# Opening rebuilt, bias rows in 16 transfers instead of 48, and odd prompt heads' transposes copied by VectorE

## The reference

```python
for layer in range(2):
    x = x + 0.5 * swiglu(rms_norm(x, g1), w_gate, w_up, w_down)      # FFN 2816
    h = rms_norm(x, g)
    y = mla_mixer(h, ...) if layer == 0 else sliding_window_gqa(h, kv, rel_bias, sinks)
    x = x + y
    x = x + 0.5 * swiglu(rms_norm(x, g2), w_gate2, w_up2, w_down2)
    if layer == 0:
        kv = rms_norm(x, kv_norm) @ w_kv_shared
y = rms_norm(x, final_norm)
```

## Time and profile before

| what | value |
|---|---|
| median of 3 runs | 2559.46 us (2558.42 to 2562.18) |
| the profiled execution | 2553.65 us, its span 2551.8 us |
| TensorE busy | 2463.2 us, 97% of the span, 16448 matmuls |
| VectorE, ScalarE, GpSimd busy | 46%, 30%, 35% |
| chain that ended last | TensorE 89%, VectorE 5%, ScalarE 2%, issue 2%, GpSimd 1%, SyncE's queue 1%, DMA 1% |
| TensorE's longest waits | 15.4 us (VectorE, `wa`), 11.4 us (GpSimd, `wa`), 4.4 us (VectorE, `split`), 2.7 us (VectorE, `split`) |

### The profile page before, as it was taken

One profiled execution on the slowest core, in us unless ns is written; L12 is line 12 of the kernel. 1 busy time (PEld: TensorE's weight loads), 2 busy tenths in 40 slices (PEclk: granted clock), 3 DMA queues, 4 the chain that ended last, 5 costly groups with the idle time before them and its releaser, 6 DMA issues.

```text
span 2551.8 us, 42418 instructions
## 1 busy us (share of the span) xinstructions
PE 2463.2 (97%) x16448; PEld 2348.0 (92%) x16448; DVE 1161.3 (46%) x2375; ACT 763.5 (30%) x1496; POOL 893.3 (35%) x602
## 2 busy tenths in 40 slices
PE   6999999999999999999999899999999999999997
PEld 6999999987666999999999899999996899999997
DVE  6443434656355353434345334343455454434435
ACT  4222222422246222121214322212145442222223
POOL 3423333444113333333323433333355243333332
PEclk9999999999999999999999999999999999999998
DMA  4312123244242122222221322222222122222211
GB/s 144 95 59 92 59 90 75 85 151 157 87 142 87 53 81 75 74 74 74 74 74 34 125 75 74 74 74 74 74 104 100 42 75 92 66 82 69 79 49 42
DMA packets 73311, 210.80 MB, mean 83 GB/s; under 512 B 8385, under 2 KB 22753, under 8 KB 72449
## 3 DMA queue, kind: packets, MB, share of 16 engines
q1 hardware_dynamic: 73216, 209.55, 25.9%
HBM read 191.22 MB, written 18.30 MB: 82 GB/s over the span
## 4 chain that ended last, share of the span: by engine, by line
PE 89%; DVE 5%; issue 2%; ACT 2%; POOL 1%; SPq 1%; DMA 1%; DVEq 0%; ACTq 0%; POOLq 0%
PE psa L355 17%; PE psa L356 17%; PE psa L357 17%; PE psb L355 10%; PE psb L356 10%; PE psb L357 10%; DVE split L436 1%; PE psb L980 1%; PE psa L1116 1%; PE psa L949 1%; PE psb L1135 1%; PE psb L1123 1%; SPq L1923 1%; DVE work L403 1%; PE psa L950 1%
## 5 line engine op out<-in xcount | busy, mean ns | idle before, releaser
L355 PE MATMUL psa<-split,wa 128*128 128x320 f32 (+1 forms) x3072 | 954.2, 311 | 48.2 <-DVE wa L2069 15.4
L357 PE MATMUL psa<-split,wa 128*128 128x320 f32 x3056 | 943.3, 309 | 0.0
L356 PE MATMUL psa<-split,wa 128*128 128x320 f32 x3056 | 943.2, 309 | 0.0
L342 POOL TENSOR_TENSOR wb<-raw,wb 128x1024 fp32r<-128x1024 f32 (+1 forms) x100 | 237.5, 2375 | 1193.4 <-ACT wb L334 1193.4
L355 PEld LDWEIGHTS psa<-split,wa 128*128 128x128 f32 x3072 | 580.3, 189 | 53.5 <-DVE wa L2069 15.4
L356 PEld LDWEIGHTS psa<-split,wa 128*128 128x128 f32 x3056 | 576.5, 189 | 1.3 <-issue 0.6
L357 PEld LDWEIGHTS psa<-split,wa 128*128 128x128 f32 x3056 | 576.1, 189 | 0.0
L342 POOL TENSOR_TENSOR wa<-raw,wa 128x1024 fp32r<-128x1024 f32 x207 | 494.0, 2407 | 172.3 <-ACT wa L334 172.3
L355 PE MATMUL psb<-acts,wb 128*128 128x320 f32 x1440 | 446.4, 310 | 1.0 <-DVE xs L633 0.8
L633 DVE SCALAR_TENSOR_TENSOR xs<-psb,xs 128x320 f32<-128x320 f32 x720 | 341.4, 488 | 229.7 <-PE psb L357 229.7
L357 PE MATMUL psb<-acts,wb 128*128 128x320 f32 x1440 | 443.5, 308 | 0.0
(11 more groups left out here) (217 smaller groups left out, 2135.6 us busy)
## 6 DMA issues: line engine op xcount, KB each, us to landing
raw<-in_w SPq DMA_DIRECT2D x310, 512.0 KB, 3.9
park<-xs SPq DMA_DIRECT2D x2, 2560.0 KB, 9.1
work<-in_c_latT SPq DMA_DIRECT2D x8, 512.0 KB, 3.9
work<-in_c_lat SPq DMA_DIRECT2D x8, 512.0 KB, 3.6
xs<-in_x SPq DMA_DIRECT2D x2, 1280.0 KB, 9.1
xs<-park SPq DMA_DIRECT2D x1, 2560.0 KB, 13.4
xs<-park SPq DMA_DIRECT2D x2, 1280.0 KB, 5.6
y_out<-xs SPq DMA_DIRECT2D x8, 320.0 KB, 3.1
```

Source lines behind the costliest of these rows:

```text
L342: nc.gpsimd.tensor_tensor(lo[:, 0:n], raw[:, (p % RAW_SLOTS) * PIECE:(p % RAW_SLOTS) * PIECE + n], hi[:, 0:n].bitcast(F32), ALU.subtract). ...
L355: nc.tensor.matmul(ps, w[0], xx[1], start=first, stop=False)
L356: nc.tensor.matmul(ps, w[1], xx[0], start=False, stop=False)
L357: return nc.tensor.matmul(ps, w[0], xx[0], start=False, stop=last)
```

## The change

The opening: consts lose their last two columns and go first, alone; two weight pieces follow, then half 0 of x in two parts, half 1, the third and fourth piece, and only then `ones`. ScalarE copies one zeroed column first (`act_start`), splits two pieces, makes all 16 high parts of x and then all 16 squares, with the further splits between. VectorE (`dve_start`) splits the first five pieces and makes all adds; GpSimd begins with the sixth piece. `pe_bias` comes right after group (0,0), `dve_bias` ahead of VectorE's adds. The groups of unit 1 use the banks of `psb`, and both norm sums lie in group (1,0).

The bias rows: 8 transfers for the sampled rows, 4 heads each, and 8 for the band rows, 2 heads each. The prompt heads: the copy of odd tasks is VectorE's, with a semaphore of its own.

```diff
@@ semaphores, waits
-AHEAD = (0, 2)
+AHEAD = (2,)
-                eng.wait_ge(consts_in, 32)
-            if i % DT == 0:
-                eng.wait_ge(x_in[i // DT], 16)
+                eng.wait_ge(consts_in, 16)
+            if i % 4 == 0 and i < 12:
+                eng.wait_ge(x_in[i // 4], 16)
@@ new functions
+    def act_start(act):
+
+        act.wait_ge(warm_zero, 1)
+        nc.scalar.activation(consts[:, CONST_COLS - 1:CONST_COLS], consts[:, CONST_COLS - 2:CONST_COLS - 1], ACT.Copy).then_inc(warm_copy, 1)
+        split_hi(act, 0, 0)
+        split_hi(act, 0, 1)
+        for i in range(N_OUT):
+            norm_hi(act, 0, i)
+        for i in range(4):
+            norm_square(act, 0, i)
+        split_hi(act, 0, 2)
+        split_hi(act, 1, 0)
+        for i in range(4, DT):
+            norm_square(act, 0, i)
+        split_hi(act, 1, 1)
+        for i in range(DT, DT + 4):
+            norm_square(act, 0, i)
+        split_hi(act, 1, 2)
+        act_std(act, 0, 0)
+        for i in range(DT + 4, N_OUT):
+            norm_square(act, 0, i)
+        split_hi(act, 2, 0)
+        act_std(act, 0, 1)
+        split_hi(act, 2, 1)
+
+    def dve_start(dve):
+
+        nc.vector.memset(consts[:, CONST_COLS - 2:CONST_COLS - 1], 0.0).then_inc(warm_zero, 1)
+        early = [(0, 0), (0, 1), (0, 2), (1, 0), (1, 1)]
+
+        def split(p):
+            dve.wait_ge(w_hi, p + 1)
+            hi, lo = slots(*early[p])
+            nc.vector.tensor_tensor(lo, raw[:, lot(p % RAW_SLOTS, PIECE)], hi.bitcast(F32), ALU.subtract).then_inc(w_lo, 1)
+        split(0)
+        split(1)
+        for i in range(N_OUT):
+            dve_norm(dve, 0, i)
+        dve_bias(dve)
+        for i in range(DT):
+            norm_add(dve, 0, i)
+        for p in range(2, 5):
+            split(p)
+        for i in range(DT, N_OUT):
+            norm_add(dve, 0, i)
+        dve_rstd(dve, 0, 0)
@@ pe_gate_up, pe_ffn
-            bank_free = [(up_out, at(it, 8, GU * i + 2 * off + h - 1))]
+            bank_free = [(x_upd, BIAS_GROUPS), (n_std, 2 * h)][:h + 1] if i == 0 and it is None and off == 1 else [(up_out, at(it, 8, GU * i + 2 * off + h - 1))]
+        banks = psb[:, 2 * h:2 * h + 2, 0:HT] if i == 0 and it is None and off == 1 else psa[:, 2 * h:2 * h + 2, 0:HT]
-            if i != 2 and it is None and (off, h, k) in ((0, 1, 3), (1, 0, 1))[i == 3:]:
+            if i != 2 and it is None and (off, h, k) in (((1, 0, 0), (1, 0, 5)) if i == 0 else ((0, 1, 3), (1, 0, 1))[i == 3:]):
+                if i == 0 and (off, h) == (0, 0):
+                    pe_bias(pe)
@@ prompt heads
-                pe.wait_ge(a_ptd, t - 1)
+                pe.wait_ge(a_ptd_odd if t % 2 else a_ptd, t // 2)
-            pe.wait_ge(a_ptd, 2 * s + 2)
+            pe.wait_ge(a_ptd, s + 1)
+            pe.wait_ge(a_ptd_odd, s + 1)
             copy(2 * s)
-            copy(2 * s + 1)
+        def copy_odd(t):
+
+            dve.wait_ge(a_tr, t + 1)
+            if t >= 4:
+                dve.wait_ge(a_pv, t - 3)
+            n = P * (i_of(t) + 1)
+            nc.vector.tensor_copy(p_pt[:, t % 4, 0:n], psb[:, 1, 0:n]).then_inc(a_ptd_odd, 1)
@@ dve_prompt, after the two maxima of a step
+            copy_odd(2 * s + 1)
@@ transfers
-        sp.dma_start(consts[:, :], a["consts"]).then_inc(consts_in, 16)
-        sp.dma_start(ones[:, :], a["ones"]).then_inc(consts_in, 16)
-        for h in range(2):
-            sp.dma_start(x[:, :, half(h)], a["x"][:, :, half(h)]).then_inc(x_in[h], 16)
-            if h == 0:
-                load_piece(sp, 0, 0)
-                load_piece(sp, 0, 1)
+        sp.dma_start(consts[:, 0:CONST_COLS - 2], a["consts"][:, 0:CONST_COLS - 2]).then_inc(consts_in, 16)
+        load_piece(sp, 0, 0)
+        load_piece(sp, 0, 1)
+        for n, (d, h) in enumerate(((0, 0), (4, 0))):
+            sp.dma_start(x[:, d:d + 4, half(h)], a["x"][:, d:d + 4, half(h)]).then_inc(x_in[n], 16)
+        sp.dma_start(x[:, :, half(1)], a["x"][:, :, half(1)]).then_inc(x_in[2], 16)
         load_piece(sp, 0, 2)
         load_piece(sp, 1, 0)
+        sp.dma_start(ones[:, :], a["ones"]).then_inc(ones_in, 16)
-    def bias_rows(h):
-        first = h * CHUNK * RELS + CHUNK - 1
-        return a["l_park"][first:first + CHUNK * (RELS - 1)].rearrange("(q w) -> q w", w=RELS - 1)
+    def bias_rows(h, n, rows):
+
+        by_head = a["l_park"].rearrange("(h w) -> h w", w=CHUNK * RELS)[h:h + n, CHUNK - 1:CHUNK - 1 + rows * (RELS - 1)]
+        return by_head.rearrange("h (q w) -> h q w", w=RELS - 1)
-        for h in range(NH):
-            g, r = h // REP, h % REP
+        for g in range(KVH):
             for b2 in range(2):
-                sp.dma_start(w_sbias[b2 * HD + r * SQ:b2 * HD + (r + 1) * SQ, g, :], bias_rows(h)[0:SQ, 0:SKEYS]).then_inc(wsb_in, 16)
+                sp.dma_start(w_sbias[lot(b2, HD), g, :], bias_rows(REP * g, REP, SQ)[:, :, 0:SKEYS]).then_inc(wsb_in, 16)
-        for h in range(NH):
-            g, r = h // REP, h % REP
-            sp.dma_start(w_bias[lot(r % 2, CHUNK), 2 * g + r // 2, :], bias_rows(h)[:, 0:BAND]).then_inc(wb_in, 16)
+        for n in range(NH // 2):
+            sp.dma_start(w_bias[:, n, :], bias_rows(2 * n, 2, CHUNK)[:, :, 0:BAND]).then_inc(wb_in, 16)
@@ the engines' programs
-        pool_norm(pool, 0, 1)
-        pool.wait_ge(w_lo, 2)
-        split_lo(pool, 0, 2)
+        pool.wait_ge(w_lo, 5)
         pool_ffn(pool, 0)
```

More of the change, by code:

```diff
@@ L242, in program @@
         "consts_in", "bias_out", "parked", "x_back", "tables_in", "rope_in", "ident_in"))
-    x_in = [sem(f"x_in{h}") for h in range(2)]
+    x_in = [sem(f"x_in{h}") for h in range(3)]
+    ones_in = sem("ones_in")
     landed = [sem(f"w_landed{i}") for i in range(RAW_SLOTS)]
@@ L481, in act_table @@
             act.wait_ge(warmed, n)
+        else:
+            act.wait_ge(warm_copy, 1)
         nc.scalar.activation(consts[:, CONST_COLS - 1:CONST_COLS], eps, ACT.Sqrt).then_inc(warmed, 1)
@@ L506, in pe_gate_up @@
                 pe.wait_ge(n_lo, 16 * N_FFN[i] + h * DT + k + 1)
-            if i != 2 and it is None and (off, h, k) in ((0, 1, 3), (1, 0, 1))[i == 3:]:
+            if i != 2 and it is None and (off, h, k) in (((1, 0, 0), (1, 0, 5)) if i == 0 else ((0, 1, 3), (1, 0, 1))[i == 3:]):
                 if i:
                     pe.wait_ge(x_upd, OUT_BASE[f"ffn{i}"])
-                pe_norm_sum(pe, N_FFN[i], 1 - h)
+                if i == 0:
+                    pe.wait_ge(ones_in, 16)
+                pe_norm_sum(pe, N_FFN[i], k // 5 if i == 0 else 1 - h)
             xx = sp_hi[:, k, half(h)], sp_lo[:, k, half(h)]
-            mm3(psa[:, 2 * h, 0:HT], tiles(u, k), xx, k == 0, k == DT - 1)
-            last = mm3(psa[:, 2 * h + 1, 0:HT], tiles(u, DT + k), xx, k == 0, k == DT - 1)
+            mm3(banks[:, 0, :], tiles(u, k), xx, k == 0, k == DT - 1)
+            last = mm3(banks[:, 1, :], tiles(u, DT + k), xx, k == 0, k == DT - 1)
         last.then_inc(gu_mm, 1)
@@ L564, in tile_step @@
             follows = u0 + off + 1 < len(UNITS)
-            if it is None and off == 0 and i != 2:
+            if i == 0 and it is None and off < 2:
+                pass
+            elif it is None and off == 0 and i != 2:
                 act_std(act, N_FFN[i], 1)
@@ L570, in tile_step @@
             early = it is None and off == 0 and i != 2
-            if early:
+            if early and i:
                 split_hi(act, u0 + 1, 2)
@@ L586, in pool_ffn @@
         for off in range(2):
-            split_lo_unit(pool, u0 + off + 1)
+            for j in range(2 if i == 0 and off == 0 else 0, 3):
+                split_lo(pool, u0 + off + 1, j)
         with pool.Fori(0, FFN_LOOPS - 1) as it:
@@ L612, in dve_scaled @@
             dve.wait_ge(act_split, at(it, 8, n - 1))
-        nc.vector.tensor_tensor(gt[:, h, :], psa[:, 2 * h, 0:HT], rstd[:, half(h)], ALU.mult).then_inc(gate_out, 1)
-        nc.vector.tensor_tensor(ut[:, h, :], psa[:, 2 * h + 1, 0:HT], rstd[:, half(h)], ALU.mult).then_inc(up_out, 1)
+        banks = psb[:, 2 * h:2 * h + 2, 0:HT] if i == 0 and it is None and off == 1 else psa[:, 2 * h:2 * h + 2, 0:HT]
+        nc.vector.tensor_tensor(gt[:, h, :], banks[:, 0, :], rstd[:, half(h)], ALU.mult).then_inc(gate_out, 1)
+        nc.vector.tensor_tensor(ut[:, h, :], banks[:, 1, :], rstd[:, half(h)], ALU.mult).then_inc(up_out, 1)
     def dve_product(dve, i, it, off, h):
@@ L2063, in _ @@
     def _(dve):
-        for i in range(4):
-            dve_norm(dve, 0, i)
-        for j in range(2):
-            dve.wait_ge(w_hi, j + 1)
-            hi, lo = slots(0, j)
-            nc.vector.tensor_tensor(lo, raw[:, lot(j, PIECE)], hi.bitcast(F32), ALU.subtract).then_inc(w_lo, 1)
-        for i in range(4, DT):
-            dve_norm(dve, 0, i)
-        dve_norm_ahead(dve, 0)
+        dve_start(dve)
         dve_ffn(dve, 0, N_MLA)
```

24 lines of the change are left out of this document (9 added, 15 removed).

## The result

The changed kernel took 2531.74 us (median of 4 runs, 2530.83 to 2532.57) and the kernel before 2558.94 (4 runs, 2554.99 to 2562.18): ratio 0.9894, 95% interval [0.9877, 0.9911], or 23 to 31 us less. A second measurement, beside three other kernels, gave 2533.15 against 2557.73: ratio 0.9914 [0.9897, 0.9930], 18 to 26 us less. The profiled execution took 2532.57 (span 2530.7) where that of before took 2553.65 (span 2551.8).

The account below looks back on a forecast made before the run. TensorE, busy 97% of the span, was taken as the bound, so only its gaps and lower clock could give time. 14.2 + 12.5 + 0 + 0 = 26.7 us off 2559.46 gave 2532.8, predicted as 2533; range 2525 to 2547 at 0.8.

Parts of the forecast that it names:

- The two large terms: The gains forecast for the opening, 14.2 us, and for the sampled bias rows at ffn2, 12.5 us.
- Opening: Kernel start: unit 2 of the first FFN starts at 44.2 us, not 58.41; gain 14.2 us, bounds 10 to 17.
- The two ties: Opening, VectorE just behind TensorE: TensorE 0.6 us late for `w_lo`, another 0.5 for the sums of half 1.
- D: Opening gives only 10 us: second tie fails, clock falls again, GpSimd holds up VectorE at the scalings; 2537 us, chance 0.23.
- Sampled bias rows: At ffn2's unit 1: 8 issues replace 32, weights issued 11.5 us earlier, TensorE's gap goes; gain 12.5 us, bounds 9 to 13.1.
- the sum's 11.6 and 1.4: Inside the sampled rows' gain at ffn2: 11.6 us for TensorE's gap, 1.4 for the lower clock after it.
- Band rows: Window stage: 8 issues replace 16, about 5.5 us earlier for what follows on SyncE, whose user isn't waiting; value 0.
- Rival B: Sampled and band transfers use only four and two DMA engines, delaying ffn2's weights and VectorE's band rows; 2537 us, chance 0.30.
- Prompt heads: Prompt stage: 32 of 64 copies move from ScalarE to VectorE, which gets some 14 us more; value 0, bounds +3 to -3.

Follow-up runs that it names:

- exchanging two lines: Kernel before, with the sampled rows' 32 transfers issued behind the weights of ffn2's second unit, not ahead: 2543.10 against 2555.18 us, ratio 0.9955.
- The four parts alone: Kernel before with one part each: opening 2544.87 us, sampled rows 2545.01, band rows 2557.09, prompt copies 2556.09.

## Why the prediction came out right

2533 was forecast and 2531.74 and 2533.15 were measured, inside 2525 to 2547. The two large terms carried it; point by point:

**Opening: 14.2 us forecast, 13.8 in the pair of profiles, 12.8 between the means of five and seven profiles.** Nearly every step is in the trace: first matmul 10.14 (10.4), bias matmuls 19.89 (19.8), the bias copy 20.20 (20.3), `w_lo` 28.2 (28.0), the sum of half 1 at 34.32 (33.4), unit 2 at 44.61 (44.2). The one step that was off is the pace of the sums: the prediction adds up durations of 0.48 us, but from one sum to the next it takes 0.58, since each waits for the one before. That is 0.6 us for each seven. GpSimd's split was counted rightly, as one sum of 2.5 us and six of the usual length; the trace has one of 2.49. The two ties held: waits of 0.51 and 0.85 us, forecast 0.6 and 0.5. D's mechanism, GpSimd holding up the scalings, didn't come: beside its splits at 33.92 and 36.69 the scalings at 36.27 and 36.68 took 0.49 and 0.48 us. One reading of the prediction was wrong: the 0.27 us between the first matmuls of the kernel before aren't in the granted clock, which reads 1.00 in 16 to 20 us; the sum uses only the 0.27 and stands. What the prediction couldn't see is that its starting point, 58.41, was 1.5 to 2.1 us later than in the four other profiles of that code, for 1.6 us of it by one more fall of the clock.

**Sampled bias rows: 12.5 forecast, 11.7 measured** by the stretch in the profiles. The issues cost 5.88 us, forecast 5.5. The cause as stated, weights behind 17 us of issues, is shown by exchanging two lines. (By its own rows the sum's 11.6 and 1.4 are 11.4 and 1.5; that moves it by 0.1.)

**Band rows: value 0 forecast, and in this kernel 1.1 to 1.4 lost.** The failed step is "8 issues in place of 16, about 5.5 us earlier for what is behind them on SyncE": they were 3.9 us longer, the weights took 4.8 us longer from issue to split, and that split came from 9.2 us ahead of the first score (1892.16 and 1901.36 in the kernel before) to 0.5. The prediction's user of these weights "isn't waiting", and neither is it here; what waits behind their split is ScalarE's table load and exponentials. Rival B's mechanism is what happened: two engines, 36 to 37 ns a row (768 bytes at 21 GB/s), the low end of its 36 to 71. At that price the rows were still in time, so the band part of B cost 1.1 to 1.4 us, where B as a whole was priced 4 to 5 us above A. It wasn't the band rows that became late, as B had it, but the weights queued behind them.

**Prompt heads: 0 forecast, 0 measured** (81.19 us of the stage against 81.17). VectorE got 7.7 us more there, not some 14.

**Sum.** With 12.8 + 11.7 - 1.2 = 23.3 the stretches give 3.4 us less than the 26.7 forecast and lie inside both measured intervals (23 to 31 at the edge, 18 to 26). That the forecast's total fell so near has some luck in it: the late unit 2 in the profile of before and the small losses were overlooked together. In the total the runs can't tell 23 from 27. The four parts alone, by span x clock, come to 10.2 + 7.1 + 0.1 + 1.6 = 19.0 with errors of 0.6 to 0.9 each; the whole gave 14.4 in the second measurement (standard error 1.1), and the first four runs of the changed kernel (2509.0, standard error 1.3) some 16. That the parts add up to more than the whole is within two to three of their errors and not explained. In the second measurement the mean span was 23 us shorter; the rest of these 23 us is a higher mean clock, 0.9915 against 0.9882. The gap in ffn2 is one place of it (0.83 and 0.94 above); at which others the clock stayed up isn't settled, since in the profiles its dips move from one execution to the next.

**What stays open.** Why two engines carried the same rows at 46 to 47 GB/s in the kernel with the band rows alone and at 41 to 43 in both profiles of the changed kernel. By size this difference, 1.8 us over the rows, would turn a hidden cost into a wait; no run shows it alone. And why the clock rises after 13 matmuls of the opening in one profile and after 23 in another, which is a microsecond of unit 2's start.

## What to carry to other kernels

Before merging DMAs to save issues, look at the outermost index of the merged one: put a long one there (rows, not heads), or fewer transfers become slower ones, and whatever is queued behind them can pay before the data itself does. First try to exchange two lines in the queue: where small transfers stand ahead of weights, the order alone can bring the whole gain. And take the yardstick of a gain from several profiles: one profile's start of a stage was 2 us off, most of it by the clock.

## What the runs showed of the hardware

Transfers with 2 outermost ran at 41 to 47 GB/s in all, with 4 at 82 to 91, with 64 at 161. As the two engines fell behind, SyncE's own issues grew from 0.52 us (the shortest) to 2.07 (the median) and 2.72 (the longest), so badly spread transfers also hold up the queue of the engine that issues them:

```profile
L1995 SPq DMA_DIRECT2D work<-l_park x8: 523/2070/2722, 1855.3 to 1868.2; - x8
```

With the outermost index exchanged the median was 0.61 us. GpSimd's split of 2.56 us stretched one of VectorE's sums out of SBUF from 0.49 to 2.49 us and left the others alone. In the kernel before, TensorE's clock was lower behind the 11.44 us without work: 0.54 granted in 1413 to 1417, and 0.83 over the 30 us around it.
